# A four-stage transformer forward pass on one core: the RMS norms' high and low parts taken straight from the transpose bank, adds by halves, and four conditioning slots moved ahead of the attention's projection

## What is computed

```python
x = x + even_mixer(rms_norm(x, e_ln_mix))          # RG-LRU and RWKV7, then the projection e_out
x = x + swiglu(rms_norm(x, e_ln_ffn))              # e_ffn, 2816 hidden columns
x = x + diff_attention(rms_norm(x, o_ln_mix))      # qkv, 8 heads, projection o_out
x = x + moe(rms_norm(x, o_ln_ffn))                 # 8 experts, top 2, 3584 hidden columns
for l in (0, 1):                                   # conditioned layers over x and 256 context rows
    mod = adaLN_table(cond) @ W[l]                 # scales, shifts and gates of the layer
    x = x + gate * attention_l(mod_norm(x), ctx)   # l0_out, l1_out
    x = x + gate * swiglu_l(mod_norm(x))           # l0_ffn, l1_ffn
return x
# rms_norm(x, g) = x * rsqrt(mean(x * x) + 1e-6) * g
```

## Time and profile before

| | |
|---|---|
| Time, median of 3 runs | 2724.45 us (2723.17 to 2728.71) |
| The profiled execution | 2722.08 us, span 2720.0 us |
| TensorE's mean granted clock | 0.993 of full speed |
| PE, PEld, DVE, ACT busy | 96%, 84%, 70%, 52% of the span |
| Mean DMA rate | 226 GB/s, 615 MB moved |

### The profile page before, as it was taken

One profiled execution on the slowest core, in us unless ns is written; L12 is line 12 of the kernel. 1 busy time (PEld: TensorE's weight loads), 2 busy tenths in 40 slices (PEclk: granted clock), 3 DMA queues, 4 the chain that ended last, 5 costly groups with the idle time before them and its releaser, 6 DMA issues.

```text
span 2720.0 us, 46988 instructions
## 1 busy us (share of the span) xinstructions
PE 2622.2 (96%) x18619; PEld 2273.2 (84%) x18619; DVE 1901.7 (70%) x2847; ACT 1406.0 (52%) x2256; POOL 0.2 (0%) x4
## 2 busy tenths in 40 slices
PE   8899999988999999999999999999999999999998
PEld 7675998846999999999999988954999999865897
DVE  3755555747888888888888888774655655664654
ACT  2412333334777777777777777272443443353432
POOL 0000000000000000000000000000000000000000
PEclk9999999998999999999999999999999999999999
DMA  6536442575999899989898988020645552321541
GB/s 261 232 144 251 186 184 77 211 318 207 334 338 339 340 342 336 341 336 342 332 347 327 350 324 319 16 94 11 248 183 186 186 186 94 114 103 70 193 185 55
DMA packets 57000, 615.07 MB, mean 226 GB/s; under 512 B 6448, under 2 KB 6704, under 8 KB 6704
## 3 DMA queue, kind: packets, MB, share of 16 engines
q1 hardware_dynamic: 56448, 610.20, 59.5%
q10 hardware_dynamic: 432, 3.15, 0.3%
HBM read 612.28 MB, written 1.05 MB: 225 GB/s over the span
## 4 chain that ended last, share of the span: by engine, by line
PE 83%; DVE 10%; ACT 3%; DMA 2%; issue 2%; DVEq 0%; SPq 0%; ACTq 0%
PE psum L1677 8%; PE psum L1679 8%; PE psum L1678 8%; PE psum L322 6%; PE psum L324 6%; PE psum L323 6%; PE psum L512 4%; PE psum L1706 4%; PE psum L1708 4%; PE psum L1707 4%; PE psum L337 3%; PE psum L338 3%; PE psum L339 3%; PE psum L664 2%; DMA ring<-stream_dram 2%
## 5 line engine op out<-in xcount | busy, mean ns | idle before, releaser
L406 DVE TENSOR_TENSOR r_high<-ring,r_high 128x1024 fp32r<-128x1024 f32 x936 | 1090.1, 1220 | 115.8 <-ACT r_high L368 115.0
L368 ACT ACTIVATE r_high<-ring 128x1024 fp32r<-128x1024 f32 x624 | 626.3, 1059 | 6.4 <-DMA ring<-stream_dram 6.4
L1677 PE MATMUL psum<-r_high 128*128 128x256 f32 x1792 | 510.9, 285 | 13.0 <-DVE r_high L1903 12.9
L1679 PE MATMUL psum<-r_high 128*128 128x256 f32 x1792 | 507.7, 283 | 0.0
L1678 PE MATMUL psum<-r_high 128*128 128x256 f32 x1792 | 507.4, 283 | 0.0
L322 PE MATMUL psum<-r_low,r_high 128*128 128x256 f32 x1408 | 399.8, 284 | 1.7 <-DVE r_high L482 1.7
L324 PE MATMUL psum<-r_low,r_high 128*128 128x256 f32 x1408 | 398.4, 283 | 0.0
L1677 PEld LDWEIGHTS psum<-r_high 128*128 128x128 f32 x1792 | 341.8, 191 | 37.7 <-DVE r_high L1903 13.4
L1678 PEld LDWEIGHTS psum<-r_high 128*128 128x128 f32 x1792 | 342.0, 191 | 4.4
L1679 PEld LDWEIGHTS psum<-r_high 128*128 128x128 f32 x1792 | 342.3, 191 | 0.0
L372 ACT ACTIVATE r_high<-ring 128x1024 fp32r<-128x1024 f32 x312 | 329.4, 1056 | 0.0
(11 more groups left out here) (509 smaller groups left out, 4224.7 us busy)
## 6 DMA issues: line engine op xcount, KB each, us to landing
ring<-stream_dram SPq DMA_DIRECT2D x384, 1536.0 KB, 8.2
arena<-bias_dram ACTq DMA_DIRECT2D x2, 1024.0 KB, 8.0
pack<-pack_dram SPq DMA_DIRECT2D x1, 1664.0 KB, 16.6
const<-const_dram SPq DMA_DIRECT2D x1, 1060.0 KB, 13.1
x<-x_dram SPq DMA_DIRECT2D x1, 1024.0 KB, 5.1
xc<-ctx_dram SPq DMA_DIRECT2D x1, 1024.0 KB, 24.5
arena<-band_dram ACTq DMA_DIRECT2D x1, 1024.0 KB, 5.1
out_dram<-x SPq DMA_DIRECT2D x1, 1024.0 KB, 3.9
```

The costliest lines, as they stand in the source:

```text
L368: act.activation(w_hi[:, i % 2, part * D:part * D + D], slot_of[r][:, part * D:part * D + D], ACT.Copy)\
L406: ins = dve.tensor_tensor(lo, slot_of[r][:, o:o + D], hi.bitcast(f32), SUB)
L1677: pe.matmul(dst, xe_hi[:, k, :], hi, start=(k == 0), stop=False)
L1679: ins = pe.matmul(dst, xe_lo[:, k, :], hi, start=False, stop=(k == KD - 1))
```

## The change

**Norms 1 and 2.** hT is gone from them. ACT takes the high part straight from the transposes in PSUM, times the gain, by eight copies of 128 by 256 (rows_hi_act); DVE takes the low part by eight scalar_tensor_tensor of the same shape, PSUM times gain minus high part (rows_lo_dve). Two halves of four blocks are signalled apart, and for qkv PE waits for each half of x_lo by itself. DVE's filler ahead of them is shorter: in norm 1 the third part of the first weight slot's split and the tables of layer 0 come after x_lo, in norm 2 one qkv piece instead of two stands ahead. **Squares and roots of norms 1, 2, 3 and 7** move to ACT (squares_act, tokens_root_act; mean and epsilon are folded into the root), and the additions into x are made by halves of 512 columns. In norm 7 the third part of the first split also comes after x_lo.

**Conditioning slots.** Layer 1's first four slots come ahead of qkv's in the ring: PE does three of them right after e_ffn, ahead of norm 2's transposes, and one behind them. The units 0 to 8 of the attention carry slots 4 to 12, the units 9 to 12 none; three still come at the end. ACT saves the early four's sum, DVE adds it back after the units. SP's loop over that part of the ring is written out.

**Projections.** In the last tile of each of out_tile_pe's projections (o_out, l0_out, l1_out) all eight blocks of the contraction are done for the first half of the columns, then all for the second, and the slots are given free in the second pass. **The end**: multiply and add by halves, and four transfers of 128 by 512 instead of one of 128 by 2048. The counts of idle_pe fall: 8 to 6 in norm 1, 9 to none and 5 to 2 in norm 2, and by one at two smaller places.

```diff
-    ("qkv", QKV // COLS), ("ada1", ADA_SLOTS), ("o_out", 3),
+    ("ada1", ADA_SLOTS), ("qkv", QKV // COLS), ("o_out", 3),
...
+ADA_EARLY = 4
+RING_AT = {_name: FIRST[_name] for _name in FIRST}
+RING_AT["qkv"] = FIRST["ada1"] + ADA_EARLY
+RING_AT["ada1_rest"] = RING_AT["qkv"] + QKV // COLS
+DRAM_AT = [*range(FIRST["ada1"], FIRST["ada1"] + ADA_EARLY), *range(FIRST["qkv"], FIRST["o_out"]),
+           *range(FIRST["ada1"] + ADA_EARLY, FIRST["qkv"])]
...
+        def squares_act(act):
+            act.activation(eps_root, eps_col, ACT.Sqrt)
+            for j in range(NT):
+                roots[0] += 1
+                squares[0] += 1
+                act.wait_ge(sem("rms_in"), roots[0])
+                act.activation(xn[:, j, :], x_tm[:, j, :], ACT.Square, accum_out=ss[:, j:j + 1]).then_inc(sem("x_squares"), 1)
+        def tokens_root_act(act, n):
+            act.wait_ge(sem("x_squares"), squares[0])
+            act.activation(inv_rms[:, 0:n], ss[:, 0:n], ACT.Sqrt, scale=1.0 / D, bias=eps_col).then_inc(sem("rms_out"), 1)
...
+        def rows_hi_act(act, k, gain, hi, name):
+            for c in range(KD):
+                if c % 2 == 0:
+                    act.wait_ge(sem("norm_tr"), 4 * k + c // 2 + 1)
+                ins = act.activation(hi[:, c, :], chunk_ps(c), ACT.Copy, scale=gain(c))
+                if c % 4 == 3:
+                    ins.then_inc(sem(name), 1)
+        def rows_lo_dve(dve, src, gain, hi, lo, hi_name, hi0, lo_name, filler, rstd_ctx=None):
+            rstd = tokens_root_dve(dve, NT if rstd_ctx is None else 2 * NT)
+            dve.tensor_scalar(rows_tm[:, 0, :], src[:, 0, :], rstd[:, 0:1], None, MUL)
+            step(dve, dve.tensor_scalar(rows_tm[:, 1, :], src[:, 1, :], rstd[:, 1:2], None, MUL), "norm_xn")
+            if rstd_ctx is not None:
+                step(dve, dve.tensor_copy(rstd_ctx, rstd[:, NT:2 * NT]), "dve_step")
+            filler()
+            for half in range(2):
+                dve.wait_ge(sem(hi_name), hi0 + half + 1)
+                for c in range(4 * half, 4 * half + 4):
+                    ins = dve.scalar_tensor_tensor(lo[:, c, :], chunk_ps(c), gain(c), hi[:, c, :].bitcast(f32), MUL, SUB)
+                if half or lo_name == "px_lo":
+                    ins.then_inc(sem(lo_name), 1)
+            dve.sem_inc(sem("norm_half"), 1)
+            dve.sem_inc(sem("norm_hT"), 1)
...
+                    if marks and 2 * j + hf < 2 * tiles - 1:
+                        ins.then_inc(sem("out_tile"), 1)
...
-            ffn_x_lo_dve(dve, swiglu, q, 0)
+            split_dve(dve, swiglu, ffn_at(name, q, 0), 0, 2, 3)
             split_dve(dve, swiglu, ffn_at(name, q, 1), 1)
+            if meanwhile:
+                meanwhile()
...
+        def add_tokens(dve, q, dst, scale_row=None, tmp=None, name="rms_in"):
             for j in range(NT):
-                src = psum[:, 2 * j:2 * j + 2, :].rearrange("p b n -> p (b n)")
-                if scale_row is not None:
-                    step(dve, dve.tensor_tensor(tmp, src, scale_row, MUL), "dve_step")
-                    src = tmp
-                step(dve, dve.tensor_tensor(dst[:, j, :], dst[:, j, :], src, ADD), "dve_step")
+                for hf in range(2):
+                    if 2 * j + hf < 2 * NT - 1:
+                        out_tile_dve(dve)
+                    else:
+                        dve.wait_ge(sem("ffn_dn"), (q + 1) * NB_FFN)
+                    add_half_dve(dve, dst, j, hf, 0, scale_row, tmp, name if hf or name != "rms_in" else "dve_step")
...
+            for hfs in ((0,), (1,)) if last else ((0, 1),):
+                for k in range(KD):
+                    n = n0 + k // 3
+                    if first and k % 3 == 0:
+                        slot_ready(pe, n)
+                    w = slot_of[n % RING]
+                    for hf in hfs:
+                        o = (k % 3) * D + hf * 512
+                        ins = pe.matmul(psum[:, 2 * j + hf, :], lhs(k)[:, j * P:(j + 1) * P], w[:, o:o + 512],
+                                        start=(k == 0), stop=(k == KD - 1))
+                    if last and 1 in hfs and (k % 3 == 2 or k == KD - 1):
+                        ins.then_inc(w_used[n % RING], 1)
+                if 0 in hfs:
+                    ins.then_inc(sem("out_tile"), 1)
...
+        def add_half_dve(dve, dst, j, hf, bank, scale_row, tmp, name):
+            cols = slice(hf * 512, hf * 512 + 512)
+            src = psum[:, bank + 2 * j + hf, :]
+            if scale_row is not None:
+                step(dve, dve.tensor_tensor(tmp[:, cols], src, scale_row[:, cols], MUL), "dve_step")
+                src = tmp[:, cols]
+            step(dve, dve.tensor_tensor(dst[:, j, cols], dst[:, j, cols], src, ADD), name)
...
-            starts = (0,) if l else (0, ADA_SPLIT)
+            starts = (0, ADA_EARLY if l else ADA_SPLIT)
...
-                if s in f["x_ready"]:
-                    pe.wait_ge(sem("px_lo"), f["x_ready"][s])
                 for half in range(2):
+                    if s == 0:
+                        pe.wait_ge(sem("px_lo"), half + 1)
                     i = 2 * s + half
...
-            act.wait_ge(sem("norm_tr"), 12)
-            for half, ready in ((slice(0, 4), "norm_half"), (slice(4, 8), "norm_hT")):
-                act.wait_ge(sem(ready), 3)
-                act.activation(x_hi[:, half, :], hT[:, half, 0:T], ACT.Copy).then_inc(sem("px_hi"), 1)
+            first_pieces_act(act, qkv_split, 0, 1)
+            rows_hi_act(act, 2, lambda c: vec("o_ln_mix", c), x_hi, "px_hi")
+            first_pieces_act(act, qkv_split, 1, qkv_split["n"])
+            ada_rows_act(act, 1, ADA_EARLY)
...
-                if n < ADA_1:
-                    ada_pe(pe, 1, n, n + 1)
+                if ADA_EARLY + n < ADA_1:
+                    ada_pe(pe, 1, ADA_EARLY + n, ADA_EARLY + n + 1)
...
-            with sp.Fori(1, min(G_MOE, g_end)) as g:
+            n0, n1 = FIRST["ada1"], FIRST["o_out"]
+            with sp.Fori(1, n0 // RING) as g:
                 for r in range(RING):
                     sp.wait_ge(w_used[r], g)
                     sp.dma_start(slot_of[r], stream_in[g * RING + r]).then_inc(w_ready[r], 16)
+            for n in range(n0 // RING * RING, G_MOE * RING):
+                sp.wait_ge(w_used[n % RING], n // RING)
+                sp.dma_start(slot_of[n % RING], stream_in[DRAM_AT[n - n0] if n0 <= n < n1 else n])\
+                  .then_inc(w_ready[n % RING], 16)
             for r in range(RING):
                 sp.wait_ge(w_used[r], G_MOE)
...
-            sp.wait_ge(sem("x_final"), 1)
-            sp.dma_start(out, x[:, :]).then_inc(sem("stored"), 16)
-            sp.wait_ge(sem("stored"), 16)
+            for b in range(2 * NT):
+                sp.wait_ge(sem("x_final"), b + 1)
+                sp.dma_start(out[:, 512 * b:512 * b + 512], x[:, 512 * b:512 * b + 512]).then_inc(sem("stored"), 16)
+            sp.wait_ge(sem("stored"), 16 * 2 * NT)
...
-            norm_pe(pe, 1)
+            norm_pe(pe, 1, rows_tm)
             ada_tr_pe(pe, 0)
-            idle_pe(pe, 8)
+            idle_pe(pe, 6)
             ffn_pe(pe, 0, "e_ffn")
-            idle_pe(pe, 9)
-            norm_pe(pe, 2)
-            idle_pe(pe, 5)
+            ada_pe(pe, 1, 0, ADA_EARLY - 1)
+            norm_pe(pe, 2, rows_tm)
+            ada_pe(pe, 1, ADA_EARLY - 1, ADA_EARLY)
+            idle_pe(pe, 2, 5)
             diff_pe(pe)
-            idle_pe(pe, 4, 5)
+            idle_pe(pe, 3, 5)
...
+            def ahead():
+                ada_rows_dve(dve, 0)
+                first_split_dve(dve, "e_ffn", 0)
+            rows_lo_dve(dve, x_tm, lambda c: vec("e_ln_ffn", c), x_hi, x_lo, "x_hi", 0, "x_lo", ahead, ctx_rstd)
+            def tables():
+                ada_mods_dve(dve, 0)
+                ada_z_dve(dve, 1)
+            ffn_dve(dve, 0, "e_ffn", None, tables)
+            add_tokens(dve, 0, x_tm)
+            rows_lo_dve(dve, x_tm, lambda c: vec("o_ln_mix", c), x_hi, x_lo, "px_hi", 0, "px_lo",
+                        lambda: first_pieces_dve(dve, qkv_split, 0, 1))
```

More of the change, by code:

```diff
@@ L325, in gate_up_pe, with down_pe @@
             ins.then_inc(sem(s + "_gu"), 1)
-        def down_pe(pe, f, at, i, first, last):
+        def down_pe(pe, f, at, i, first, last, marks=False):
             r, turn, blk = at
@@ L398, in blocks_act, with split_dve @@
                 stage(i)
-        def split_dve(dve, f, at, i):
+        def split_dve(dve, f, at, i, first=0, end=3):
             r, turn, blk = at
-            for part in range(3):
+            for part in range(first, end):
                 o = part * D
@@ L503, in out_tile_pe @@
-        def out_tile_pe(pe, n0, lhs, j, first, last):
[L505 to L508, removed]
-                w = slot_of[n % RING]
-                for hf in range(2):
-                    o = (k % 3) * D + hf * 512
-                    ins = pe.matmul(psum[:, 2 * j + hf, :], lhs(k)[:, j * P:(j + 1) * P], w[:, o:o + 512],
```

(26 more changed lines are left out.)

136 lines of the change are left out of this document (69 added, 67 removed).

## The result

The changed kernel took 2712.5 us (median of 5, 2709.9 to 2714.3); the runs of before beside it 2727.6, the ratio 0.9946 [0.9931, 0.996]. It is faster, and 0.5 us above the forecast range. A repetition gave 2711.7 and 0.9943 [0.993, 0.9956]. Before's median over the repeated comparisons is 2726 to 2729: the 2724.45 that the forecast was put on was a low draw of three, and the profiled execution (2722.1) lower still.

What follows compares the result with a forecast made beforehand. PE bounds the experts' stage, slot transfers the attention's units, and DVE and ACT chains the norms. Terms summed to -19.8 us on the 2724.45 median, giving 2704.5; the forecast range was 2700 to 2709, at 0.53.

Steps and rivals of the forecast that it cites:

- norm 1: From e_out to e_ffn: PE starts at 245.5 instead of 249.75, with the fillers deciding; -4.2 us.
- norm 2, to qkv's first product: From e_ffn to qkv: x_lo's first half and PE at 449.9 against 454.91; -5.0 us.
- low clock behind it: Behind norm 2's pause: clock 0.56 for 3.9 us, a 1.7 us loss kept in both kernels, so no term.
- attention: Units 9 to 12 carry no slot and take 2.32 us instead of 3.78 each; -5.8 us, bounds 2 and 5.8.
- norm 3, norm 7: Shorter add, square and mean steps, and in norm 7 the third split part leaves the chain; -0.8 and -2.4 us.
- projections by halves: Last tile frees slot 0 later, delaying l0_ffn's first down product from 1920.27 to 1921.4; +1.2 us, bounds 0.5 and 1.6.
- the end: After the last matmul: additions by halves -1.3 us and a smaller last store -1.5 us; -2.8 us together.
- a second stretch: Behind norm 2's longer bare pause: another half-clock stretch would cost +1.7 us, making norm 2 give -3.3.
- l0_ffn's term: At l0_ffn's start: first down product later because its transfer waits for slot 0; +1.2 us, lower bound 0.5.
- what is late is the slot, not the rows: At norm 2: qkv's first slot lands at 444.7, while DVE would be ready for a piece at 441.
- Rival (a): At norm 2: qkv's first slot lands at 12.0 us instead of 6.3, total -14.2, 2710.3 us; chance 0.15.
- The store's last quarter: At the kernel's end: the last 256 KB store takes 2.4 us, against 3.9 for 1 MB; -1.5 us.

## Why the prediction missed

By its own steps, on the two profiles of equal clock (spans 2724.7 and 2707.3):

| Step | forecast | measured |
|---|---|---|
| norm 1 | -4.2 | -4.2 |
| norm 2, to qkv's first product | -5.0 | -5.3 |
| low clock behind it | 0 | +1.4 |
| attention | -5.8 | -5.8 |
| norm 3, norm 7 | -0.8, -2.4 | -0.8, -2.4 |
| projections by halves | +1.2 | +0.5 |
| a slot's landing in layer 1 | 0 | +1.5 |
| the end | -2.8 | -2.7 |
| everything else | 0 | about +0.4 |
| sum | -19.8 | -17.4 |

The mechanisms of the edited steps held, and so did most of their sizes. Norm 1's is in part luck: against the profile that the forecast was made on it gave 3.2. It had the fillers as what decides, which the run with four fillers bears out, but at full clock.

**The step that failed** is the low clock put at nothing: "I keep that loss in both kernels, so it is no term". The first profile of before had the low stretch behind qkv's first product, its second did not; with the bare pause of 3.1 to 3.6 us all five profiles have it. So the loss is not one that both kernels always have, and the change adds 1.4 us against an execution of before without it. Filling the pause removed it. The prediction had named the longer pause as what speaks against the change, priced a second stretch at +1.7, and left it out. The Trainium skill (TensorE: Matmul & The Clock Gate, section Part 1: The HAM clock gate) has an idle engine fall to half clock, which pointed the right way. The trace agrees: 0.50 for 3.4 us behind the pause of 3.46.

**A wait that the sum did not have.** All its terms were places that an edit touches. The landing of one slot in layer 1 grew from 6.2 to 7.7 us, in code that the change leaves alone, and cost 1.5 in both pairs of profiles.

**The base.** The sum was put on a median of three. Before's own runs span 2721.7 to 2732.7, with mean clocks from 0.987 to 0.993, the slower ones at the lower clock. Against the 2727.9 of eleven runs the forecast would have been 2708, and the shortfall is some 4 us, not 8: that base is the largest single part of the miss. Of the 4, the table has 2.4. The rest, between spans of two executions and medians of many, stays open. The first product is a candidate: it began at half clock, 1.9 us, in 7 of the 11 profiles with the changed norms and in none of the 4 with the old ones. So are stretches at the attention's end, in 6 of 12 profiles of kernels with early slots and in none of the 3 without; but counted over the whole attention a low stretch stands in 9 of the 12 and 2 of the 3. That the change brings either is not shown.

**The size of l0_ffn's term**: 1.2 forecast, 0.5 measured (0.3 in the first profile). The table load went ahead of the wait, which the prediction had as its lower bound.

What it did not see is that its own sentence, "what is late is the slot, not the rows", was worth 4.7 us in an easy change: with the faster norm the moved slots pushed qkv's first slot out of the ring and cost at norm 2, with the clock, what they gave in the attention. Three of them keep both. Rival (a), a landing of 12.0 us, did not occur: ACT began on the first slot 6.5 us after its issue. The store's last quarter landed in 2.5 us, where the prediction took 2.4.

## What to carry to other kernels

A prefetch ring is a budget: work moved into a pause should leave the slot that the next stage needs first in its place. When a chain gets shorter, look at which transfer has become its last wait. And price PE's bare pauses as a term with a clock of its own: fillers that end just before the product cost nothing here. A forecast from one profile needs that profile's clock beside the clock of the runs. Last, look also at the waits for transfers in stages that no edit touches: one of them grew by 1.5 us here.

## What the runs showed of the hardware

Executions of one kernel differ by up to 11 us in 2722 with their mean granted clock (0.987 to 0.993): low stretches at 0.50 appear also where PE is busy throughout, as under norm 1's fillers (3.40 of 3.40 us at 243.9). The very first product can run at half speed (matmuls 0.43 us apart against 0.22) where the profile's clock column says 1.00. Eight scalar_tensor_tensor of 128x256 from PSUM took 0.40 us each (3.22), less than the 0.485 of the earlier trace rows out of SBUF, and ACT's copies, which ran beside them on other banks for 1.1 us, were not slowed (3.00 against 3.03). A store of 256 KB landed in 2.5 us, one of 1 MB in 3.9. Layer 1's slot of 1.5 MB landed in 6.1 to 6.6 us, and in 7.0 to 7.7 where a packet of the instruction queue fell into it.
